# The last third of a mixing stage, with several steps of its written order moved

## The reference

```python
mod = jax.nn.silu(c) @ w_ada + b_ada                      # shift, scale, gate of both halves
h = rmsnorm(x, norm1_g) * (1.0 + sc1) + sh1
xr, gr, q, k, v, o, ig, fg, u = jnp.split(h @ w_in, ...)
y_a = rglru(causal_dwconv(xr), ...) * jax.nn.gelu(gr)
# mLSTM, in 8 chunks of 128 tokens, 4 heads of 96:
num = S @ v + inter * (C @ q);  den = sum(S) + inter * (n @ q)
h = num / max(|den|, exp(-m_t));  C = decay * C + (w * v).T @ k
y_b = jax.nn.sigmoid(o) * rmsnorm(h, mlstm_norm_g)
# pooling: 4 groups of 64 features, windows 2, 4, 8, 16
y_c = ((window_sum(u) / count - u) @ pool_w) * pool_scale
x = x + gt1 * (concatenate([y_a, y_b, y_c]) @ w_out)
x = x + gt2 * (square(relu((rmsnorm(x, norm2_g) * (1 + sc2) + sh2) @ w_ff1)) @ w_ff2)
y = rmsnorm(x, final_g)
```

## Time and profile before

| | |
|---|---|
| runs, median of 3 | 1176.22 us (1174.27 to 1178.18) |
| the profiled execution | 1175.78 us, its span 1174.0 us |
| PE busy in the span | 1124.6 us (96%) |
| DVE, ACT, POOL busy | 792.8, 473.4, 346.9 us |
| PE busy, 340 to 350 us | 6.28 of 10 us, mean granted clock 0.68 |
| PE busy, 350 to 360 us | 10.00 of 10 us, clock 0.98 |
| loads of ADA tiles from ACT's queue | 28 of 512 KB, median 4.1 us to landing |

### The profile page before, as it was taken

One profiled execution on the slowest core, in us unless ns is written; L12 is line 12 of the kernel. 1 busy time (PEld: TensorE's weight loads), 2 busy tenths in 40 slices (PEclk: granted clock), 3 DMA queues, 4 the chain that ended last, 5 costly groups with the idle time before them and its releaser, 6 DMA issues.

```text
span 1174.0 us, 19681 instructions
## 1 busy us (share of the span) xinstructions
PE 1124.6 (96%) x7237; PEld 1077.3 (92%) x7237; DVE 792.8 (68%) x1319; ACT 473.4 (40%) x780; POOL 346.9 (30%) x275
## 2 busy tenths in 40 slices
PE   4799999999989999999999999999999999999997
PEld 1598888888979999899999999999999999999996
DVE  4561455478775434678578878778778788788546
ACT  5551355655456344642233332332432433433431
POOL 0442011201434357764032022132131231231352
PEclk9699999998989999999999999999999999999998
DMA  8912523566523722111111111202102202111104
GB/s 302 326 57 88 142 90 126 177 180 218 176 87 113 269 90 73 54 55 37 37 36 55 54 37 55 71 18 71 56 16 75 68 18 72 53 50 58 37 1 145
DMA packets 67846, 109.85 MB, mean 94 GB/s; under 512 B 6435, under 2 KB 42567, under 8 KB 67399
## 3 DMA queue, kind: packets, MB, share of 16 engines
q1 hardware_dynamic: 57574, 84.88, 22.0%
q10 hardware_dynamic: 10208, 24.12, 6.6%
HBM read 96.81 MB, written 12.18 MB: 93 GB/s over the span
## 4 chain that ended last, share of the span: by engine, by line
PE 82%; DVE 9%; ACT 3%; DMA 2%; issue 1%; POOL 1%; SPq 1%; ACTq 0%; POOLq 0%; DVEq 0%
PE D L2407 7%; PE D L2409 7%; PE D L2408 7%; PE D L2591 6%; PE D L2593 5%; PE D L2592 5%; PE X L2593 5%; PE X L2591 5%; PE X L2592 5%; PE X L2663 5%; PE X L2664 5%; PE X L2665 5%; PE D L2663 2%; PE D L2665 2%; PE D L2664 2%; DMA RAWW<-in_WADA 2%
## 5 line engine op out<-in xcount | busy, mean ns | idle before, releaser
L2407 PE MATMUL D<-H_hi,W_hi 128*128 128x344 f32 x472 | 158.6, 336 | 3.7 <-POOL H_lo L1087 3.1
L2409 PE MATMUL D<-H_hi,W_lo 128*128 128x344 f32 x472 | 152.4, 323 | 0.0
L2408 PE MATMUL D<-H_lo,W_hi 128*128 128x344 f32 x472 | 152.4, 323 | 0.0
L1087 POOL TENSOR_TENSOR Y_lo<-FU,Y_hi 128x344 fp32r<-128x344 f32 (+3 forms) x84 | 100.1, 1194 | 154.2 <-ACT Y_hi L1521 88.5
L1082 POOL TENSOR_TENSOR W_lo<-RAWW,W_hi 128x1024 fp32r<-128x1024 f32 x25 | 61.6, 2465 | 182.5 <-ACT W_hi L1234 182.2
L1087 POOL TENSOR_TENSOR Y_lo<-EY,Y_hi 128x344 fp32r<-128x344 f32 (+1 forms) x24 | 38.3, 1598 | 216.3 <-ACT Y_hi L1521 144.5
L2407 PEld LDWEIGHTS D<-H_hi,W_hi 128*128 128x128 f32 x472 | 90.5, 192 | 11.8 <-issue 7.6
L2408 PEld LDWEIGHTS D<-H_lo,W_hi 128*128 128x128 f32 x472 | 90.3, 191 | 0.9 <-issue 0.5
L2409 PEld LDWEIGHTS D<-H_hi,W_lo 128*128 128x128 f32 x472 | 90.2, 191 | 0.0
L2215 DVE SCALAR_TENSOR_TENSOR X<-X,MOD 128x344 f32<-128x344 f32 (+1 forms) x138 | 75.7, 566 | 9.2 <-PE X L2665 9.0
L2663 PE MATMUL X<-Y_hi,W_hi 128*128 128x344 f32 x252 | 80.7, 320 | 0.0
(11 more groups left out here) (416 smaller groups left out, 3455.1 us busy)
## 6 DMA issues: line engine op xcount, KB each, us to landing
RAWW<-in_W SPq DMA_DIRECT2D x76, 512.0 KB, 3.6
RAWW<-in_WADA ACTq DMA_DIRECT2D x28, 512.0 KB, 4.1
RAWW<-in_WADA SPq DMA_DIRECT2D x20, 512.0 KB, 8.0
RAWW<-in_W ACTq DMA_DIRECT2D x18, 512.0 KB, 3.7
X0T<-in_x SPq DMA_DIRECT2D x3, 1376.0 KB, 12.8
out_y<-OUTN SPq DMA_DIRECT2D x24, 172.0 KB
X<-in_x SPq DMA_DIRECT2D x8, 344.0 KB, 5.3
NM<-nm_d SPq DMA_DIRECT2D x8, 256.0 KB, 5.3
```

Of the source, the lines that this page charges most:

```text
L1087: nc.gpsimd.tensor_tensor(lo_v, fu_v, hi_v.bitcast(F32), ALU.subtract).then_inc(lo_ready, 1)
L2407: T.matmul(out, w_h, hi[:, kt, a:b], start=(kt == 0), stop=False)
L2408: T.matmul(out, w_h, lo[:, kt, a:b], start=False, stop=False)
L2409: one = T.matmul(out, w_l, hi[:, kt, a:b], start=False, stop=(kt == KT - 1))
```

## The change

Only the string is changed. No instruction of arithmetic is added or taken away.

```diff
-D:13:1 S:5 ADA:21:1 POOLV:0 YS POOLS:0 POOLD:0 SX:5 W:15 YSD AB:5 NU:5 HN:5 HM:5
-D:13:2 ADT:21 R:59 U:5 CN:5
-D:14:0 Y:2 ADM:21 EX:6 YD:2
-D:14:1 ADA:22:0 S:6 SX:6 R:61 AB:6 ADA:22:1 Y:3 POOLV:1
-D:14:2 POOL:0:0 POOLS:1 NU:6 YD:3 R:60 POOLY:0:0 POOL:0:1 ADT:22 POOLY:0:1 HN:6 LD:7 POOL:0:2 POOLD:1 POOLY:0:2 ADM:22
-    HM:6
-D:15:0 U:6 Y:4 POOL:1:0 R:62 CN:6 POOLY:1:0 ADA:23:0 EX:7 POOL:1:1 W:16 R:64 YD:4
+D:13:1 S:5 ADA:21:1 POOLV:0 YS POOLS:0 POOLD:0 SX:5 YSD AB:5 NU:5 HN:5 W:15
+D:13:2 ADT:21 ADM:21 HM:5 R:59 U:5 CN:5
+D:14:0 Y:2 EX:6 YD:2
+D:14:1 ADA:22:0 S:6 SX:6 R:61 AB:6 NU:6 ADA:22:1 Y:3 POOL:0:0 POOLY:0:0 POOL:0:1 POOLY:0:1 POOLV:1
+D:14:2 POOL:0:2 POOLS:1 POOLY:0:2 YD:3 R:60 POOLD:1
+D:15:0 ADT:22 ADM:22 HN:6 LD:7 U:6 HM:6 POOL:1:0 Y:4 R:62 CN:6 POOLY:1:0 ADA:23:0 EX:7 POOL:1:1 W:16 R:64 YD:4
 D:15:1 POOLY:1:1 S:7 SX:7 POOL:1:2 POOLY:1:2 ADA:23:1 R:63
-D:15:2 Y:5 YD:5 AB:7 NU:7 ADT:23 HN:7
+D:15:2 W:17 Y:5 YD:5 AB:7 NU:7 ADT:23 HN:7
 D:16:0 R:65 HM:7 Y:6 U:7 YD:6 CN:7 ADM:23
-D:16:1 Y:7 W:17 YD:7
+D:16:1 Y:7 YD:7
 D:16:2
```

## The result

| | before | after |
|---|---|---|
| median | 1174.74 us of 20 runs | 1177.28 us of 20 runs |
| the profiled execution | 1175.78 us, span 1174.0 | 1177.23 us, span 1175.4 |
| PE busy in the span | 1124.6 us | 1122.9 us |

The changed kernel is slower: the ratio is 1.0020, 95% interval 1.0011 to 1.0029, so +2.4 us with 1.3 to 3.4. The forecast was 1175.5 us, and no change the likeliest. The time lies in the range, but with this many runs the sign can be told, and it is the other one.

What follows compares the result with a forecast made beforehand. PE, busy 96% of the span, was taken as the bound, so only its waits and half clock could yield time. Terms 0 + 0.25 - 1.0 = -0.75 us gave a median of 1175.5 us, range 1171.8 to 1178.6.

Steps and rivals of the forecast that it cites:

- middle part: Moves of NU:6, pooling products, ADT:22 and R:60: D:15:1 ends at 360.5 against 360.25, +0.25 us.
- last weight tile: W:17 copied and split three tiles sooner: 1.51 us wait goes, about 0.35 and 0.15 come back, net -1.0 us.
- Y:2's turn and the root: ADM:21 ahead of the root's wait: Y:2 1.5 us sooner, 1.7 us wait moves to A of AB:6, gain 0.
- Numerator and pooling products: NUM ends at 336.8; sums lengthen 1.1 us; R:60 leaves 3.1 us later, takes 4.9; ADA:23:0 starts 1.3 sooner.
- queued behind: Rival, chance 0.06: R:60 queues behind OT and chunk 7 loads; over 0.3% slower from 9.2 us to landing.
- The clock: Behind ADA:23:0: 3.2 us of work at half clock from 353.9, costing 1.6 us, bounds 0 and 3.4.
- begins late: Rival, chance 0.12: half clock falls just before 353.9, all 6.8 us meet full work; 1.8 us more, 1177.3.
- first part: Moves of W:15, ADM:21 and HM:5 at Y:2 and the root: the wait moves to A, gain 0.

Runs made afterwards that it cites:

- root_part: Kernel before with only W:15 behind HN:5 and ADM:21 ahead of HM:5, as in the change; 1174.63 us, 1.0006 of before.
- no_middle_wait: Kernel before with the change's W:15, ADM:21, HM:5 and W:17 moves, plus GpSimd waiting for HN:7 before the last weight tile's split; 1174.74 us, 1.0011 of before.
- w17_back: Changed kernel with W:17 put back beside Y:7; 1177.58 us, 1.0023 of before.
- after_wait: Changed kernel with GpSimd waiting until HN:7 is done on VectorE before splitting the last weight tile; 1176.68 us, 1.0017 of before.
- no_middle: Kernel before with the change's W:15, ADM:21, HM:5 and W:17 moves; numerator, pooling products, ADT:22 and R:60 as before; 1175.37 us, 1.0009 of before.
- load_early: Changed kernel with R:60, the load for ADA:23:0, issued ahead of POOL:0:0; 1177.49 us, 1.0024 of before.
- nu6_part: Kernel before with only NU:6, the pooling products, ADT:22 and R:60 moved as in the change; 1178.64 us, 1.0023 of before.
- w17_only: Kernel before with W:17 alone moved ahead of Y:5; 1175.7 us, 1.0000 of before.
- w17_wait: Kernel before with W:17 moved ahead of Y:5 and GpSimd waiting for HN:7 on VectorE before splitting this tile; 1173.75 us, 0.9984 of before.
- fixed: Changed kernel with ADA:22:1 ahead of AB:6, R:60 behind NU:6, and GpSimd's last weight split waiting for HN:7; 1173.84 us, 0.9986 of before.

## Why the prediction failed, step by step

In short: the prediction failed in two terms. The middle part was put at +0.25 us: its load landed 1.1 us later than the assumed 4.9, and half clock lay over more work. The last weight tile was put at -1.0 us, and the traces have +1.1, since GpSimd's split held two short VectorE operations.

**Y:2's turn and the root: right in the wait, doubtful in the price.** A waits 1.64 us (1.7 foreseen), and nothing is gained: alone 1.0006, within 0.0015. The possible half clock was foreseen, and 0 was taken for it since the slack would cover it. Of the seven traces with this wait of 1.64 us, six have a half clock behind it, for 3.4 us (root_part, no_middle_wait, w17_back, after_wait) or 6.8 (no_middle, load_early); only the changed kernel's has none. The three of them without the middle part are 1.03, 1.02 and 2.83 us longer to S:7 than before, so it wasn't wholly covered. Their times, 1.0006, 1.0011 and 1.0009, leave this open.

**Numerator and pooling products: right in the chain, wrong in the load.** NUM ended at 335.27, which is 15.5 us behind ADT:21 (15.6 foreseen). The sums took 8.84 us (9.0). R:60 left 27.67 us behind ADT:21, before 24.59: 3.1 us later, as said. The rule of the Trainium skill (SBUF — State Buffer, Who interferes with whom), by which each low part would be added whole, would have made the sums 10.1 us by the 1.13 of the earlier trace rows. The added time was less than half of that. The ends above (341.02 and 341.00) and the low parts, 3.60 us for two, look like two engines that hold each other by turns, as the rule has it, with the price shared between them. The load is the term that was mis-sized: it landed after 6.0 us, not 4.9. In w17_back, nu6_part and after_wait PE starts ADA:23:0 6.0, 6.0 and 6.2 us behind the issue, against 4.8 us to landing in w17_only, whose order there is that of before. So ADA:23:0 won 0.28 us, not 1.3. The step that failed is "the neighbours are there again, so I take 4.9". By the prediction's own terms the load leaves 3.1 us later but YD:3, on which its neighbours hang, only 1.7, so it had to fall behind them. The traces agree: R:60 leaves 1.1 us behind OT in all four traces of this order, and within 0.01 us of it in before, w17_only and root_part. OT and K now land after 2.8 and 3.0 us instead of 3.9 and 5.3, and R:60 pays. This is the rival "queued behind" in kind, at 1.1 us instead of its 4.3 or more. No run moves the load among its neighbours with all else equal, so the order is the likely cause and not shown to be. The wait for X3 ahead of ADT:22 (1.64 us) wasn't foreseen; it lies within the load's.

**The clock: right in this one profile, low over several.** The half clock cost 1.57 us behind ADA:23:0 (1.6 foreseen). From ADA:23:0 to S:7 w17_back, nu6_part and after_wait took 7.46, 7.20 and 7.18 us, against 5.02 at full clock: 2.2 to 2.4. With the load this makes the stretch to S:7 longer by 1.29, 2.27, 1.96 and 2.29 us in the four traces of this order, where the forecast has **+0.25**. The times agree: the middle part alone 1.0023, and it adds 0.0011 to no_middle and 0.0017 to root_part. So the half clock cost more than forecast, though not all of the rival "begins late", and the load was 1.1 us late. I had given these rivals 0.12 and 0.06 as if one of them had to do all. Which of two executions of one order gets how much half clock, the order of the steps doesn't tell.

**The last weight tile: the step that failed outright.** -1.0 was forecast, and the trace has +1.1. The wait of 1.51 went as said. But GpSimd's split made Y:7 1.87 us late, not 0.35, and the second tile 0.74, not 0.15. I had priced an overlap by one large product (1.08 for 0.56) and applied that to HN:7, whose first operations have four columns. Those took 2.41 us for 0.50, +1.91, and each ended within 0.02 us of the GpSimd operation beside it. That is what the named rule of the Trainium skill says, and the trace agrees: the first was held for the rest of W_lo, the second for the Y_lo behind it. HN:6's two, which start at 349.28 beside low parts of the pooling pieces, took 0.63 and 0.83 us instead of 0.17 each as before. All five traces with the early split and without GpSimd's wait have the long pair; the five with W:17 in its old place and the five with the wait have the short one. In the time the sign is less sure. Moving W:17 changed the ratio by 0.0000, -0.0003 and +0.0003 in three pairs (w17_only, the change against w17_back, no_middle against root_part), 0.0 in the mean. Each difference is uncertain by 0.0015 to 0.0019, and the mean by 0.0010 (1.2 us), so the times lean neither to the trace's +1.0 nor to -1.0 and exclude neither clearly. The wait for GpSimd gave back 0.0016, 0.0003, 0.0019 and -0.0002, 1.1 us in the mean, against 1.67, 1.71, 2.71 and 1.49 us in the stretches.

By the times the sum is 0.7 (first part) + 2.0 (middle, mean of three pairs) + 0.0 = 2.7 us for 2.4 measured, where 0 + 0.25 - 1.0 was forecast. Each of these terms is uncertain by about 1 us or more, so the agreement proves little. Of the waits named, those before Y:4 and ADA:23:0 were there and that before POOL:1:0 was not; the one at ADT:22 wasn't named. The two places where a resource is shared (the load among its neighbours, GpSimd beside VectorE) were priced too low.

**A better version.** w17_wait is faster than both kernels (0.9984), fixed nearly so (0.9986, up to 1.0000). no_middle_wait, which holds the same edit, is not (1.0011), so a gain of about 1 us is likely and not settled. With 13 kernels measured, one at 0.9984 is also less telling than its own interval.

## What to carry to other kernels

A product's wait removed on the busiest engine is only worth what the second chain leaves: here the load's chain and VectorE's chain ended within about half a us of each other. With the wait at ADA:23:0 removed (3.64 us), S:7 waited 3.46; with that removed too, the output projection came no sooner. Before a helper engine's long operation is moved, look for the short operations on the critical chain that it will stand beside; one wait that puts the split some 3 us later took its cost in the traces away. When a load is moved, look at what it now leaves behind, and not only at who is in flight with it. And measure in stretches from a common point of the program, where the clock is the same: behind S:7 kernels of one order repeat within 0.15 us, where medians of 12 runs scatter by 1 to 2. Ahead of S:7, where the half clock differs from one execution to the next, they differ by up to 1.8 us (no_middle and no_middle_wait), and one trace doesn't settle a term of 1 us.

## What the hardware showed unexpectedly

- Two VectorE operations of 128x4 took 1.47 and 0.94 us beside a GpSimd operation of 2.40 us, where in the other kernels the first took 0.17 to 0.34 and the second 0.17; a 128x1022 one beside low parts lost only 0.4 us (1.66 for 1.23), and a copy of two columns 0.6. In HN:7 the price was what was left of GpSimd's operation, and not a share of VectorE's.
- The half clock came in stretches of 3.4, 6.8 and, in nu6_part, 10.2 us, where both before had been 6.8. It followed a wait of 1.64 us in six of seven traces, and in the changed kernel's the same wait was followed by none. Over full work each costs half its length, and executions of the same order differed by 1 us or more.
- A load of 512 KB took 6.0 instead of 4.9 us among the same five neighbours when it left 1.1 us behind the first of them instead of with it; in all four traces of that order it took about 6.0 to 6.2.
